# First block: norms of Q, K and the delta output from compact sums, and another order of the QKV projection

## What is computed

```python
c = jax.nn.silu(dwconv_centred(qkv, conv_w)).astype(jnp.float32)
q, k, v = jnp.split(c, [DN_QK, 2 * DN_QK], axis=-1)          # 8 heads of 128
q = q * lax.rsqrt(jnp.sum(q * q, -1, keepdims=True) + EPS) * (DN_DK ** -0.5)
k = k * lax.rsqrt(jnp.sum(k * k, -1, keepdims=True) + EPS)
...
beta = jax.nn.sigmoid(bal[:, :, 0])
g = -jnp.exp(a_log) * jax.nn.softplus(bal[:, :, 1] + dt_bias)
o = chunk_gated_delta(both(q, q), both(k, k), both(v, v), ...)   # forward and backward
o = o[:Bn] + jnp.flip(o[Bn:], 1)
o = o * lax.rsqrt(jnp.mean(o * o, -1, keepdims=True) + EPS) * norm_g
o = o * jax.nn.silu(z)
```

## Time and profile before

| what | us |
|---|---|
| median of 3 runs (lowest, highest) | 2912.97 (2907.26, 2915.78) |
| the profiled execution | 2918.89 |
| its span, first to last instruction | 2917.1 |
| mean granted TensorE clock | 0.869 |

### The profile page before, as it was taken

The page is one execution under the profiler, slowest core; times in us unless marked ns, Lnnn a source line. Parts: engine busy times, 40 slices in busy tenths (PEclk is TensorE's granted clock), DMA queues, the critical chain, the costliest instruction groups (busy, mean ns, idle before and its releaser), DMA issues.

```text
span 2917.1 us, 34012 instructions
## 1 busy us (share of the span) xinstructions
PE 2371.4 (81%) x13488; PEld 2003.1 (69%) x13488; DVE 1390.1 (48%) x3171; ACT 1310.5 (45%) x2339; POOL 737.8 (25%) x615
## 2 busy tenths in 40 slices
PE   7987998969999999878786788687698878666676
PEld 6766887856884878867665777566587766565554
DVE  3564333341001133474656764545765644676444
ACT  1551112110000220466755667764557674556665
POOL 0010112110000000232334323333322423334564
PEclk9988999989999999987777898899797988776666
DMA  6221111123433577998889999999998999999997
GB/s 257 87 89 58 59 65 58 51 101 126 163 144 139 218 271 288 395 420 347 306 348 422 403 421 383 409 408 415 396 420 355 407 366 420 401 380 351 421 421 318
DMA packets 109999, 839.34 MB, mean 288 GB/s; under 512 B 12176, under 2 KB 12432, under 8 KB 13968
## 3 DMA queue, kind: packets, MB, share of 16 engines
q0 software_dynamic: 73728, 536.90, 45.6%
q1 hardware_dynamic: 36112, 300.25, 26.2%
HBM read 836.06 MB, written 1.05 MB: 287 GB/s over the span
## 4 chain that ended last, share of the span: by engine, by line
PE 50%; DMA 20%; DVE 13%; ACT 12%; issue 3%; POOL 1%; SPq 0%; DVEq 0%; POOLq 0%; ACTq 0%
DMA mem<-in_puv,mem 19%; PE psm L431 10%; PE psm L2142 7%; PE psm L439 5%; PE psm L1712 5%; DVE mem L2186 4%; ACT mem L2160 4%; PE psm L718 3%; PE psm L2017 3%; PE psm L1247 3%; PE psm L1350 2%; PE psm L1904 2%; ACT L2155 1%; PE psm L733 1%; PE psm L435 1%
## 5 line engine op out<-in xcount | busy, mean ns | idle before, releaser
L2142 PE MATMUL psm<-mem 128*128 128x128 f32 x4096 | 706.6, 331 | 365.3 <-ACT mem L2160 364.7
L2142 PEld LDWEIGHTS psm<-mem 128*128 128x128 f32 x4096 | 587.4, 172 | 480.4 <-ACT mem L2160 464.8
L2170 POOL DMA_INDIRECT mem<-in_puv,mem x512 | 618.0, 1207 | 1111.0 <-PE psm L2142 1036.0
L2186 DVE CUSTOM_DVE_ANT_0 mem<-mem 128x1024 f32<-128x1024 f32 x512 | 624.5, 1225 | 436.2 <-DMA mem<-in_puv,mem 435.4
L2160 ACT ACTIVATE mem<-mem 128x1024 f32<-128x1024 f32 x512 | 588.8, 1150 | 16.7
L431 PE MATMUL psm<-mem 128*128 128x256 f32 (+2 forms) x1504 | 352.6, 398 | 32.6 <-DVE mem L1180 17.1
L431 PEld LDWEIGHTS psm<-mem 128*128 128x128 f32 x1504 | 293.2, 198 | 91.3 <-issue 29.5
L2155 ACT ACTIVATE mem<-mem 128x1 f32<-128x1 f32 x512 | 101.8, 199 | 457.2 <-DVE mem L2186 456.3
L1712 PE MATMUL psm<-mem 128*128 128x256 f32 x1024 | 245.4, 392 | 0.5 <-ACT mem L1426 0.5
L1712 PEld LDWEIGHTS psm<-mem 128*128 128x128 f32 x1024 | 195.9, 197 | 27.7 <-ACT mem L1426 0.9
L439 PEld LDWEIGHTS psm<-mem 128*128 128x128 f32 x1408 | 178.7, 192 | 45.2 <-issue 22.0
(11 more groups left out here) (357 smaller groups left out, 2435.5 us busy)
## 6 DMA issues: line engine op xcount, KB each, us to landing
mem<-in_w2g SPq DMA_DIRECT2D x64, 1024.0 KB, 8.9
mem<-in_w SPq DMA_DIRECT2D x18, 2048.0 KB, 8.3
mem<-in_pwq SPq DMA_DIRECT2D x32, 1024.0 KB, 11.5
mem<-in_w2f SPq DMA_DIRECT2D x28, 1024.0 KB, 10.1
mem<-in_wgu SPq DMA_DIRECT2D x11, 2048.0 KB, 7.9
mem<-in_w2t SPq DMA_DIRECT2D x20, 1024.0 KB, 11.9
mem<-in_w2b SPq DMA_DIRECT2D x16, 1024.0 KB, 10.7
mem<-in_w2o SPq DMA_DIRECT2D x16, 1024.0 KB, 9.6
```

Source lines behind the costliest of these rows:

```text
L2142: m = pe.matmul(bank(6 + c // 4)[:, tsl(c % 4)], GR[n % PING][:, 1024 + c * 128:1152 + c * 128], ident, is_transpose=True, start=k == 0 an ...
L2170: po.indirect_dma_start(GR[n % PING], None, A[f"puv{i // 2}"], bass.IndirectOffsetOnAxis(ap=IX[i % 2][:, k:k + 1], axis=0)).then_inc(gsem[ ...
L2186: ve.tensor_tensor_reduce(out=GR[n % PING][:, 0:1024], in0=GR[n % PING][:, 0:1024], in1=X[:, i % 2, :], scale=1.0, scalar=0.0, op0=MUL, op ...
```

## The change

- **Q, K and V.** The projection uses four banks (`bank(p % 4)`), takes K and V first and Q last (`ORD`), and `ba` before all. Beta and g are computed at the start of the list (`qkv_ac`, `qkv_ve`). SiLU of K and V and the squares of K stand on ACT before pair 9. The first matmul of `delta` waits for the last convolution.
- **Norms of Q and K.** The sum over a head's 128 partitions is now a matmul with the head as stationary operand and one column of ones as moving operand (`sums_pe`): 16 matmuls for all heads and tokens, the result being 128 tokens x 16. The factor of K goes as -0.5 Ln of the sum into the exponent of the decay (`GCS`, `LNR`) and through a power on POOL into beta (`BK`), `RM` and `NBG`. C itself is no longer scaled. The factor of Q isn't applied at all: its square goes into the epsilon of the output's norm (`SSQ`), with 16 more such matmuls in chunk 0.
- **Norm of the output.** It is done by groups of heads: A (heads 0 to 3) after chunk 6, B (heads 4 to 7, second half of the tokens) after chunk 7, C (the other half) in `mid`. The sum is again a compact one, the power is taken on POOL, and PE spreads the row of factors to all partitions (`spread_pe`, four matmuls with the identity). `Z` gets SiLU within `fill` and then holds the result. The projection `dp` is done in two halves, over heads 0 to 3 and 4 to 7.

`delta` has 215 steps then (217 before): 10 instead of 17 ahead of the chunks, three after chunk 6 and two after chunk 7.

```diff
-        at_step = {"qkv": {4 * i: ("qkv", i) for i in R6} | {24: ("ba", 0)},
+        at_step = {"qkv": {4 * i + 1: ("qkv", i) for i in R6} | {0: ("ba", 0)},
...
+            W = slot(("ba", 0), 8, 32)
+            pe.wait_ge(*landed("ba", 0))
+            for t in R2:
+                pe.wait_ge(*UV[2 + t])
+                chain(pe, bank(2 + t)[:, 0:32], lambda k: HT[:, k, tsl(t)], lambda k: W[:, k, :], R8).then_inc(QP_.next(f"ba{t}"), 1)
+            yield
...
-                b = bank(2 + p % 2)
+                b = bank(p % 4)
                 pe.wait_ge(*landed("qkv", p // 2))
-                pe.wait_ge(*(QV[p - 2] if p >= 2 else UV[2 + p]))
+                pe.wait_ge(*(QV[p - 4] if p >= 4 else QV["ba"] if p >= 2 else UV[4 + p]))
...
         def qkv_ac(ac):
+            ac.wait_ge(*QV["ba"])
+            ac.activation(beta, BA[:, :, 0:16], ACT.Sigmoid).then_inc(DA.next("beta"), 1)
+            ac.wait_ge(*DV["ab"])
+            ac.activation(g1, g1, ACT.Exp, scale=-1.0).then_inc(oa.up(), 1)
+            ac.wait_ge(*oa.now())
+            ac.activation(g1, g1, ACT.Ln, bias=1.0).then_inc(DA.next("ln"), 1)
+            yield
             for p in range(12):
+                if p == 9:
+                    for i in R4:
+                        silu_ac(ac, 2 + i)
+                    for i in R2:
+                        ac.wait_ge(*DA["c", 2 + i])
+                        ac.activation(SQ[:, 4 * i:4 * i + 4, :], K[:, 4 * i:4 * i + 4, :], ACT.Square).then_inc(DA.next(("sq", i)), 1)
                 yield
                 ac.wait_ge(*QP_[p])
-                conv_ac(ac, C, bank(2 + p % 2), dcw, None, 2 * p).then_inc(QA.next(p), 1)
-                yield
+                conv_ac(ac, C, bank(p % 4), dcw, None, 2 * ORD[p]).then_inc(QA.next(p), 1)
+                yield
+
+        def silu_ac(ac, i):
+            c = C[:, 4 * i:4 * i + 4, :]
+            ac.wait_ge(*QV[(2 * i + 9) % 12])
+            ac.activation(c, c, ACT.Silu).then_inc(DA.next(("c", i)), 1)
...
+            ve.wait_ge(*QV["ba"])
+            ve.tensor_tensor(gg, BA[:, :, 16:32], bc(dtb, 1, 2), ADD).then_inc(ov.up(), 1)
+            ve.wait_ge(*ov.now())
+            ve.scalar_tensor_tensor(g1, gg, -1.0, gg, MUL, MAX).then_inc(DV.next("ab"), 1)
...
-                if j >= 2:
-                    pe.wait_ge(*FAc[j - 2])
+                pe.wait_ge(*(FAc[j - 2] if j >= 2 else QV[8 + j]))
...
+            ac.activation(Z, Z, ACT.Silu).then_inc(NZ.next("z"), 1)
+            yield
...
+        def sums_pe(pe, b, src, cols):
+
+            for u, (h, t) in enumerate(cols):
+                m = pe.matmul(b[:, u:u + 1], src[:, h, tsl(t)], ones[:, 0:1], start=True, stop=True)
+            return m
+
+        def spread_pe(pe, g, k):
+            if k == 0:
+                pe.wait_ge(*DO_[g, "r"])
+            b = d_free(pe, (g, f"b{k}"))
+            four(pe, b, lambda u: RR[:, 4 * k + u:4 * k + u + 1].broadcast_to((128, 128)), lambda u: ident).then_inc(DP.next((g, f"b{k}")), 1)
...
         def delta_pe(pe):
             pe.wait_ge(*RAc["i", 11])
-            pe.wait_ge(*QV["ba"])
-            for p in R8:
-                b = d_free(pe, ("n", p))
-                pe.wait_ge(*DO_["sq", p])
-                pe.matmul(b, ones, flat(SQ[:, 2 * p:2 * p + 2, :]), start=True, stop=True).then_inc(DP.next(("n", p)), 1)
-                yield
+            pe.wait_ge(*QV[11])
+            pe.wait_ge(*DA["sq", 1])
+            th = [(h, t) for t in R2 for h in R8]
+            sums_pe(pe, d_free(pe, "ssk"), SQ, th).then_inc(DP.next("ssk"), 1)
+            yield
...
-            pe.wait_ge(*DV["n", 7])
...
+                pe.wait_ge(*DV["bk"])
+                four(pe, b, lambda u: BK[:, t, r0_ + u:r0_ + u + 1].broadcast_to((128, 128)), lambda u: ident).then_inc(DP.next((c, "bb")), 1)
...
+                if c == 0:
+                    b = d_free(pe, (c, "ssq"))
+                    pe.wait_ge(*DO_["qs", 3])
+                    sums_pe(pe, b, SQQ, th).then_inc(DP.next((c, "ssq")), 1)
...
+                for g in NORM.get(c, []):
+                    hs, ts = HEADS[g]
+                    pe.wait_ge(*DO_[g, "sq"])
+                    sums_pe(pe, d_free(pe, (g, "ns")), SO if g == "A" else SOB, [(h, t) for t in range(len(ts)) for h in R4]).then_inc(
+                        DP.next((g, "ns")), 1)
+                    yield
+                    for k in range(len(ts)):
+                        spread_pe(pe, g, k)
+                        yield
...
         def delta_ac(ac):
-            for p in R8:
-                ac.wait_ge(*DP["n", p])
-                if p >= 2:
-                    ac.wait_ge(*DV["n", p - 2])
-                ac.activation(RT[:, p % 2, :], d_bank(("n", p)), ACT.Sqrt, bias=epsc).then_inc(DA.next(("rt", p)), 1)
-                yield
+            ac.wait_ge(*DV["ssk"])
+            ac.activation(LNK, SSK, ACT.Ln).then_inc(DA.next("lnk"), 1)
+            yield
...
+            z = Z[:, hs, cols]
+            ve.scalar_tensor_tensor(z, OD[:, hs, cols], dnn, z, MUL, MUL).then_inc(DV.next((g, "oz")), 1)
+            ve.wait_ge(*DP[g, "ns"])
+            ve.scalar_tensor_tensor(by(RR[:, 0:n], 4), by(d_bank((g, "ns"))[:, 0:n], 4), 1.0 / 128, SSQ[:, ts[0]:ts[-1] + 1, hs],
+                                    MUL, ADD).then_inc(DV.next((g, "rr")), 1)
+            yield
+            for k, t in enumerate(ts):
+                z = Z[:, hs, tsl(t)]
+                ve.wait_ge(*DV[g, "oz"])
+                ve.wait_ge(*DP[g, f"b{k}"])
+                ve.tensor_tensor(z, z, by(d_bank((g, f"b{k}")), 128), MUL).then_inc(DV.next((g, f"y{k}")), 1)
...
         def delta_ve(ve):
-            for p in R8:
-                R = RT[:, p % 2, :]
-                cv = flat(C[:, 2 * p:2 * p + 2, :])
-                ve.wait_ge(*DA["rt", p])
-                ve.reciprocal(R, R).then_inc(ov.up(), 1)
-                ve.wait_ge(*ov.now())
-                ve.scalar_tensor_tensor(cv, cv, 128 ** -0.5 if p < 4 else 1.0, R, MUL, MUL).then_inc(DV.next(("n", p)), 1)
-                yield
+            ve.wait_ge(*DP["ssk"])
+            ve.tensor_scalar(SSK, by(d_bank("ssk")[:, 0:16], 8), 1.0, 1e-6, MUL, ADD).then_inc(DV.next("ssk"), 1)
+            yield
             ve.wait_ge(*DP["gc"])
-            ve.wait_ge(*DV["gg"])
             ve.tensor_copy(GC, by(d_bank("gc")[:, 0:32], 16)).then_inc(DV.next("gc"), 1)
+            ve.wait_ge(*DA["lnk"])
+            ve.wait_ge(*DV["gc"])
+            ve.tensor_scalar(LNR, LNK, -0.5, None, MUL).then_inc(ov.up(), 1)
+            ve.wait_ge(*ov.now())
+            ve.tensor_tensor(nh(GCS), nh(GC), bc(LNR, 2, 2), SUB).then_inc(DV.next("gs"), 1)
+            ve.wait_ge(*DO_["rk"])
+            ve.tensor_tensor(nh(BK), nh(beta), bc(RK, 2, 2), MUL).then_inc(DV.next("bk"), 1)
             ve.wait_ge(*DA["nbg"])
-            ve.scalar_tensor_tensor(NBG, NBG, -1.0, beta, MUL, MUL).then_inc(DV.next("nbg"), 1)
-            yield
-            for x in R8:
-                if x % 2 == 0:
-                    ve.wait_ge(*DP[x, "vk"])
...
-                    e = ve.tensor_scalar(sl("DEC")(u), d_bank((c, "bc"))[:, tsl(u)], GC[:, t, r0_ + u:r0_ + u + 1], 0.0, SUB, MIN)
+                    e = ve.tensor_scalar(sl("DEC")(u), d_bank((c, "bc"))[:, tsl(u)], GCS[:, t, r0_ + u:r0_ + u + 1],
+                                         LNR[:, t, hq * 4 + u:hq * 4 + u + 1], SUB, MIN)
...
         def delta_po(po):
-            po.wait_ge(*RO[11])
-            for p in R8:
+            for p in R4:
                 po.wait_ge(*DA["c", p // 2])
                 c = C[:, 2 * p:2 * p + 2, :]
-                po.tensor_tensor(SQ[:, 2 * p:2 * p + 2, :], c, c, MUL).then_inc(DO_.next(("sq", p)), 1)
-                yield
-            for _ in range(9):
+                po.tensor_tensor(SQQ[:, 2 * p:2 * p + 2, :], c, c, MUL).then_inc(DO_.next(("qs", p)), 1)
...
+                for g in NORM.get(c, []):
+                    for x in dict(A=(4, 5), B=(6,))[g]:
+                        po.wait_ge(*DV[x, "od"])
+                    if g == "A":
+                        for k in R2:
+                            o2 = OD[:, 2 * k:2 * k + 2, :]
+                            e = po.tensor_tensor(SO[:, 2 * k:2 * k + 2, :], o2, o2, MUL)
+                    else:
+                        o2 = OD[:, 4:8, tsl(1)]
+                        po.wait_ge(*DP["A", "ns"])
+                        e = po.tensor_tensor(SOB, o2, o2, MUL)
+                    e.then_inc(DO_.next((g, "sq")), 1)
...
-            pe.wait_ge(*FV[3])
-            pe.wait_ge(*DV[7, "od"])
-            for p in R4:
-                pe.wait_ge(*NO["sq", p])
-                pe.matmul(bank(p), ones, flat(SQ2[:, 2 * p:2 * p + 2, :]), start=True, stop=True).then_inc(NP.next(("n", p)), 1)
-            pe.wait_ge(*NV["yd", 3])
-            for p in R4:
+            def project(p, ks):
                 W = slot(("dp", p // 2), 8, 512)
-                pe.wait_ge(*landed("dp", p // 2))
+                b = d_bank(("w", p))
```

(26 more changed lines are left out.)

197 lines of the change are left out of this document (114 added, 83 removed).

## The result

The median is 2872.4 us (2871.0 to 2874.6, four runs) against 2912.7 of before: a ratio of 0.9864, 95% interval 0.9847 to 0.9881, so 40 us less. The forecast was 2861 (2846 to 2878): the direction and the range hold, but 52 us were expected and a quarter of them are missing. The profiled execution took 2872.7 us, its span is 2870.9.

What follows compares the result with a forecast made beforehand. PE is half the chain; gains lie where PE isn't the one waited for: ahead of the chunks, Q/K/V projection, after the last chunk. 10.1 + 34.9 - 12 + 19.2 = 52 us saved, giving 2861; own range 2852 to 2870, stated range 2846 to 2878.

Steps and rivals of the forecast that it cites:

- the first rival: Projection and chunks get no shorter: recurrence hangs on DVE and ACT, ACT delays chunk 5 by 5 us; 2876, chance 0.14.
- Part 1: Projection of Q, K and V, `ba` first: no bank waits, last convolution ends at 178.6, 10.1 us earlier; bounds 0 and 13.
- Part 2: Ahead of the chunks, norms and table loads removed: 20.5 us where it was 55.4, 34.9 saved; bounds 16.6 and 25.
- the cover of that part: Ahead of the chunks: PE's 11 us of transposes and fill hide all else; without it, 3 to 5 us.
- Part 3: Chunks: added narrow sums, group A's norm and fill steps lose 12 us, bounds 7 to 18.
- no change: Chunk 5: ACT's added SiLU of Z and reordered gate work leave its time unchanged, -3 to +5 us.
- A drop of the clock: Rival: narrow matmuls keep PE's clock low; about one chunk at 1.2 GHz loses 52 us, two make 2967; chance 0.03.
- Part 4: After the last chunk, to the projection's end: 34.1 us where it was 53.3, 19.2 saved.

Runs made afterwards that it cites:

- Experiment 7: Changed kernel with the projection of Q, K and V on two banks again, new order kept: median 2881.3 us, ratio 0.9896.
- experiment 3: Changed kernel with 14 throwaway 128x256 products ahead of the first narrow sums, in PE's wait for the last convolution: median 2867.1 us, ratio 0.9843.
- experiment 5: Changed kernel with the delta steps' banks shifted, so sums over K and of g fall into PE's wait for the last convolution: 2862.0 us, ratio 0.9818.
- experiment 10: Changed kernel with delta banks shifted (sums in PE's wait for the last convolution) and narrow sums cut into pieces with fill between: 2856.9 us, ratio 0.9818.
- experiment 8: Changed kernel without the 16 narrow sums over Q in chunk 0, the epsilon made from K's sums instead: median 2866.6 us, ratio 0.9838.
- experiment 9: Changed kernel with the fill step between B's transposes and p2 exchanged with p2 in chunks 2, 3, 6 and 7 too: 2875.7 us, ratio 0.9897.
- experiment 1: Changed kernel with two fill steps exchanged so one stands between B's transposes and p2 in chunks 1 and 5: median 2869.7 us, ratio 0.9857.
- experiment 4: Changed kernel with the decay tile's minimum taken with constant 0.0 instead of a second per-partition number: median 2869.8 us, ratio 0.9853.
- experiment 6: Changed kernel with delta banks shifted (sums in PE's wait) and four fill steps exchanged in chunks 0, 1, 4 and 5: 2856.3 us, ratio 0.9801.

## Why the prediction was right, and where it was off

The stated range, 2846 to 2878, holds the measured 2872.4 only because it was drawn around the first rival too: the forecast's own range ended at 2870, and the chunks lost 21 us, outside their bounds of 7 to 18. In number the first rival (2876) is nearer than the 2861; its mechanism, a projection that is no shorter, didn't come. That the sum stayed in the range although a term didn't is luck in part.

**Part 1 was right**, number and mechanism: ACT's batch began at 136.5 (136.8 forecast), PE was done at 170.3 (170.3) and waited 7.4 (8), the last convolution ended at 177.6 (178.6). Experiment 7 gives its cause: the banks.

**Part 2 was off by 4.1 us**: 24.6 instead of 20.5. The step that failed is the price of the narrow products after the rest, where I took 5.9, 1.8 and 1.6 for the clock. I had the clock recover on the way, since the transposes of the earlier trace rows did so after 20.8 us of rest. The sums took 6.8, those of g 3.4, and what follows 14.4 instead of 12.8. By experiments 3 and 5 it is not the rest alone: the clock falls within such products even behind unbroken wide work, and experiment 10 shows that wide work in between holds it. The Trainium skill ("TensorE: Matmul & The Clock Gate", What's actually happening) has the low clock as the state that activity lifts; the trace agrees behind a rest: in the changed kernel the clock is back some 6.5 us into the wide work behind the sums. In experiment 5 it fell at 174 with PE busy throughout, so the busy share of a profile doesn't tell whether the clock stays. I had used that section for the fill behind the sums and not for the sums themselves. The power on POOL took 2.9 us and not 0.55, and lay under PE's slow work, as the cover of that part had it.

**Part 3 was off by 9.3 us**: 21.3 instead of 12 (the sums of the table). The sums of chunk 0 were sized right (3.3, experiment 8), and so was group A (6.6, chunk 6), although its wait was 1.0 and not 0.3. What was missing:
- The places without fill. I worked out how many steps of fill move, and not that seven delta steps fewer ahead of the chunks shift the pattern by which one step in twenty has none. It fell on the transposes of chunks 1 and 5: 0.9 us each (experiments 8 and 9), and 2.7 and 2.5 for the drops of the clock there, 6.9 in all, as experiment 1 gave back (3.6 + 3.3). In chunk 5 I had "no change": with the fill moved it takes 51.7, before 51.5, so the shift of ACT's tables does come to nothing. That is in part luck: the waits in that stretch are other ones (four, 6.6 us in experiment 1, for three of 6.0 before), and the low clock behind them lasts some 7 us instead of 3.
- A drop at the end of chunk 7, 1.6 (47.2 against the 45.6 of experiments 5 and 8, where it stands at the end of chunk 6). A drop of the clock was a rival only as a whole chunk at 1.2 GHz; it came as several of 1.6 to 2.7 us.
- The rest, 2.9 where I had 2.0, is what is left of the sum. The decay tile's second operand, which I took as free (1.37 instead of 1.13), is 1 us of it by experiment 4; the other 1.9 I put down to the fill steps at the end, which no run prices by themselves.

**Part 4 was nearly right**: 35.0 us (34.1). The power of group B took 1.0.

The sum: -1.0 + 4.1 + 9.3 + 0.9 = 13.3, and the projection ended 13.3 later than 622. The gain passed to the end whole, as stated. The table loads cost what the rows had, with no drain beside them: the four loads of chunk 5 took 1.28 each, and what follows three of them begins within 0.02 us (behind the fourth ACT waits for DVE).

Better than both kernels, with nothing of the work left out, are experiments 5 (0.9818 [0.9806, 0.9831]), 6 (0.9801 [0.9789, 0.9814]) and 10 (0.9818 [0.9800, 0.9836]). Open stays why the clock falls in chunk 1 of one trace and not of another with the same waits; no run here moved only the phase of the work, and each kernel has one trace.

## What to carry to other kernels

When a step is put into a woven order or taken out of it, list what each pattern step now stands beside: here a pattern that shifted by seven steps cost 7 us against one that keeps its gaps away from waits. A product of one column cost 0.22 us at the high clock and 0.43 at the low one, and a run of 24 such narrow products ended at the low one in all ten traces that have it, so cut it with wide work; but count what the wide work was to cover later. And ask of a wait whether it is for data or only for the bank: in experiment 5 the first chunk began 12 us earlier by a number in the choice of banks and the wait that went with it.

## What the hardware showed beyond that

- TensorE's granted clock went from 2.4 to 1.2 GHz while PE was busy throughout, within a run of 24 narrow products (128x1 and 128x8) that followed 34.7 us of wide ones (experiment 5), and within 16 of them in chunk 0 (experiment 6); with four to eight such products at a time between wide ones it stayed at 2.4.
- Two waits, the first of 1.1 to 1.3 us and the second of 1.5, with 0.6 us of work between them stood before a drop in 13 of 18 cases, and one wait of 1.5 alone in none of 2 (experiment 9, chunks 2 and 6).
- A power on POOL goes by its columns: 0.55, 1.01, 1.64 and 2.92 us for 1, 4, 8 and 16, which about 0.4 + 0.16 a column fits.
- Four DVE instructions of 128x128 from PSUM took 1.37 us with two per-partition numbers each, and 1.13 with one.
